# Two post norms of a transformer kernel: the residual turned ahead and the normed addend brought in by a product with a diagonal

## What is computed

```python
for layer in range(DEPTH_2):                 # 2
    h = rms_norm(x, mix_pre_g[layer])
    if layer < N_A:
        m = pool_mixer(h, pool_w[layer], pool_scale[layer])
    else:
        ...
        m = swa_sink_attention(q, kk, vv, sinks[j]) @ w_o[j]
    x = x + rms_norm(m, mix_post_g[layer])
    f = conv_glu_ffn(rms_norm(x, ffn_pre_g[layer]), ffn_w_in[layer], ffn_conv_w[layer],
                     ffn_conv_b[layer], ffn_w_out[layer])
    x = x + rms_norm(f, ffn_post_g[layer])
```

## Time and profile before

| | us |
|---|---|
| median of 3 runs | 882.49 |
| lowest, highest | 881.57, 883.0 |
| the profiled execution, device time | 882.28 |
| its span, first to last instruction | 880.4 |
| TensorE busy in the span | 854.7 (97%) |
| VectorE busy | 622.0 (71%) |
| ScalarE busy | 467.8 (53%) |
| GpSimd busy | 145.2 (16%) |
| mean granted clock of TensorE | 0.999 of full speed |

### The profile page before, as it was taken

How to read it: one execution, slowest core, us unless ns; L and a number is a source line. 1 busy time by engine, 2 the same in 40 slices (tenths; PEclk the granted TensorE clock), 3 DMA queues, 4 the chain that set the end, 5 groups by cost and what they waited for, 6 DMA issues and landing times.

```text
span 880.4 us, 15326 instructions
## 1 busy us (share of the span) xinstructions
PE 854.7 (97%) x5989; PEld 777.7 (88%) x5989; DVE 622.0 (71%) x816; ACT 467.8 (53%) x679; POOL 145.2 (16%) x132
## 2 busy tenths in 40 slices
PE   8999999998999999989999999999999999999997
PEld 8998888988999999869899999979766989999996
DVE  7887556779555555886876776877756677767776
ACT  5536765444444444465555554674656565455553
POOL 3282210017000000011122112000121121211200
PEclk9999999999999999999999999999999999999999
DMA  8953324634765555533555455435323235555541
GB/s 313 335 201 103 138 96 146 240 141 176 287 224 177 183 188 182 185 144 120 183 192 200 160 181 209 166 144 191 101 92 144 96 144 191 195 186 190 181 156 48
DMA packets 24088, 152.55 MB, mean 173 GB/s; under 512 B 2443, under 2 KB 3683, under 8 KB 7523
## 3 DMA queue, kind: packets, MB, share of 16 engines
q1 hardware_dynamic: 22672, 145.44, 47.1%
q10 hardware_dynamic: 1363, 6.37, 1.9%
HBM read 150.71 MB, written 1.09 MB: 172 GB/s over the span
## 4 chain that ended last, share of the span: by engine, by line
PE 64%; DVE 9%; ACT 3%; issue 2%; POOL 0%; DVEq 0%; POOLq 0%; ACTq 0%
PE up L990 12%; PE up L992 12%; PE up L991 12%; PE down L996 6%; PE down L997 6%; PE down L998 6%; DVE w_lo L1533 3%; PE up L1031 2%; PE down L1068 1%; PE down L1070 1%; DVE region L1949 1%; PE down L1458 1%; PE down L1216 1%; PE down L1074 1%; DVE mid L1808 1%
## 5 line engine op out<-in xcount | busy, mean ns | idle before, releaser
L1533 DVE TENSOR_TENSOR w_lo<-w,w_hi 128x2048 fp32r<-128x2048 f32 x133 | 316.8, 2387 | 63.6 <-ACT w_hi L641 63.5
L990 PE MATMUL up<-x_lo,w_hi 128*128 128x256 f32 x1240 | 354.1, 286 | 1.2 <-DVE w_lo L1533 1.2
L991 PE MATMUL up<-x_hi,w_hi 128*128 128x256 f32 x1240 | 350.8, 283 | 0.0
L992 PE MATMUL up<-x_hi,w_lo 128*128 128x256 f32 x1240 | 350.7, 283 | 0.0
L641 ACT ACTIVATE w_hi<-w 128x2048 fp32r<-128x2048 f32 x133 | 253.4, 1907 | 65.2 <-PE down L998 27.9
L990 PEld LDWEIGHTS up<-x_lo,w_hi 128*128 128x128 f32 x1240 | 237.7, 192 | 4.1 <-DVE w_lo L1533 2.1
L991 PEld LDWEIGHTS up<-x_hi,w_hi 128*128 128x128 f32 x1240 | 237.8, 192 | 1.2
L992 PEld LDWEIGHTS up<-x_hi,w_lo 128*128 128x128 f32 x1240 | 237.7, 192 | 0.0
L996 PE MATMUL down<-w_hi,mid 128*128 128x512 f32 x256 | 100.4, 392 | 3.2 <-DVE mid L1808 1.5
L997 PE MATMUL down<-w_hi,mid 128*128 128x512 f32 x256 | 100.0, 391 | 0.0
L998 PE MATMUL down<-w_lo,mid 128*128 128x512 f32 x256 | 99.6, 389 | 0.0
(11 more groups left out here) (246 smaller groups left out, 980.8 us busy)
## 6 DMA issues: line engine op xcount, KB each, us to landing
w<-w_stream SPq DMA_DIRECT2D x134, 1024.0 KB, 4.8
gates<-vec_store ACTq DMA_DIRECT2D x5, 1024.0 KB, 4.8
region<-rpb SPq DMA_DIRECT2D x2, 768.0 KB, 12.4
gates<-x_in SPq DMA_DIRECT2D x2, 512.0 KB, 3.8
result<-res SPq DMA_DIRECT2D x4, 256.0 KB, 2.0
con<-consts SPq DMA_DIRECT2D x1, 801.0 KB, 8.3
proj<-bands ACTq DMA_DIRECT2D x1, 544.0 KB, 3.7
gates<-vec_store ACTq DMA_DIRECT2D x1, 512.0 KB, 3.6
```

The costliest lines, as they stand in the source:

```text
L990: m(out_ap, w_hi[slot][:, w_cols:w_cols + P], xl, start=first, stop=False, skip_group_check=True)
L991: m(out_ap, w_hi[slot][:, w_cols:w_cols + P], xh, start=False, stop=False, skip_group_check=True)
L992: return m(out_ap, w_lo[slot][:, w_cols:w_cols + P], xh, start=False, stop=last, skip_group_check=True)
L1533: v.tensor_tensor(lo_of(n), w32[s][:, :], hi_of(n).bitcast(F32), ALU.subtract).then_inc(w_lo_ready, 1)
```

## The change

For the two post norms in `BY_DIAGONAL` the turned new residual is no longer the transpose of a sum that VectorE has made. TensorE makes the sum itself, in PSUM:
- `turn_old`: the old residual is turned by ordinary f32 products with the identity (residual chunk as the stationary operand), 16 of them. In `MIXPOST1` all 16 stand directly behind the last output product, in `MIXPOST0` between the others, since their banks are still being read.
- `diagonal(t)`: VectorE multiplies the identity by the roots of token half t, which gives `diag`, 128x128.
- `add_scaled`: the gained addend `s_tok` as stationary operand times `diag`, 16 products, accumulated onto the turned residual. `x_turned` is counted there.
- The dummy products of both places go.
- VectorE's additions into `res` (`added`) stand later in its queue: in `MIXPOST0` all four pieces behind `lower`; in `MIXPOST1` two ahead of it and two behind. They wait for `res_read`, after which TensorE no longer reads the old residual.
- ScalarE's squares of the new residual for the pre norm all stand behind the `x_hi` chunks for these two.
- In both gated layers: VectorE waits for the pre norm's root before the split of unit base + 2; the split of unit base + 3 moves from ahead of the first multiply to behind it; ScalarE's gelu of pair 0 moves ahead of the value half's product, and its split of unit base + 4 stands right behind that.

```diff
+        diag = sb("diag", [P, TT, P])
+        BY_DIAGONAL = (MIXPOST0, MIXPOST1)
...
+                if k_post not in BY_DIAGONAL:
+                    squares(0)
                 name, which = fills[0]
                 for c in range(DC):
...
-                for q in range(2):
-                    act.wait_ge(x_new, 4 * b + 2 + q + 1)
-                    mean_square(k_pre, 1, q, tok(res, 1, q), pre_squared)
+                if k_post in BY_DIAGONAL:
+                    squares(0)
+                squares(1)
...
-                    if kind == 0 and ends:
+                    if kind == 0 and (ends or j == 0):
                         gelu()
-                if not ends:
+                if j and not ends:
                     gelu()
...
+            def turned(c, t):
+
+                return turned_chunk(c)[:, t * P:(t + 1) * P]
+
+            def turn_old(c, last):
+
+                for t in range(TT):
+                    for k in (c, c + 1):
+                        ins = m(turned(k, t), res[:, t, k * P:(k + 1) * P], ident[:, :], start=(k == c and t == 0), stop=False,
+                                skip_group_check=True)
+                if last:
+                    ins.then_inc(res_read, 1)
+
+            def add_scaled(t, c):
+
+                for k in (c, c + 1):
+                    ins = m(turned(k, t), s_tok[:, t, k * P:(k + 1) * P], diag[:, t, :], start=False, stop=True,
+                            skip_group_check=True)
+                if t == 1:
+                    ins.then_inc(x_turned, 1)
+
+            def turn_scaled(k_post):
+
+                b, d = POST.index(k_post), TT * BY_DIAGONAL.index(k_post)
+                pe.wait_ge(post_gained, 4 * b + 2)
+                if k_post == MIXPOST0:
+                    turn_old(0, False)
+                    turn_old(2, False)
+                pe.wait_ge(diag_ready, d + 1)
+                add_scaled(0, 0)
+                add_scaled(0, 2)
+                pe.wait_ge(post_gained, 4 * b + 3)
+                if k_post == MIXPOST0:
+                    turn_old(4, False)
+                add_scaled(0, 4)
+                if k_post == MIXPOST1:
+                    add_scaled(0, 6)
+                pe.wait_ge(diag_ready, d + 2)
+                add_scaled(1, 0)
+                add_scaled(1, 2)
+                if k_post == MIXPOST1:
+                    pe.wait_ge(post_gained, 4 * b + 4)
+                add_scaled(1, 4)
+                pe.wait_ge(post_gained, 4 * b + 4)
+                if k_post == MIXPOST0:
+                    turn_old(6, True)
+                    add_scaled(0, 6)
+                add_scaled(1, 6)
...
-            keep_busy(aux, 13)
-            turn_new(MIXPOST0)
+            turn_scaled(MIXPOST0)
...
-            keep_busy(down[2], 6)
-            turn_new(MIXPOST1)
+            pe.wait_ge(p_ready, 32)
+            pe.wait_ge(pt_ready, 32)
+            for c in (0, 2, 4, 6):
+                turn_old(c, c == 6)
+            turn_scaled(MIXPOST1)
...
+                def diagonal(t):
+                    dve.wait_ge(rstd_ready, ROOT[k, t] + 1)
+                    v.tensor_scalar(diag[:, t, :], ident[:, :], stat[:, k, 2 + t:3 + t], None, ALU.mult)\
+                        .then_inc(diag_ready, 1)
...
+                gained(0, 0)
+                gained(0, 1)
                 if k == MIXPOST0:
-                    gained(1)
-                    added(0)
+                    gained(1, 0)
+                    diagonal(0)
+                    gained(1, 1)
+                    diagonal(1)
+                elif k == MIXPOST1:
+                    diagonal(0)
+                    variance(k, 1, (sq_ready, 4 * b + 4))
+                    gained(1, 0)
+                    diagonal(1)
+                    gained(1, 1, False)
...
             lower([("ffn_pre0", X_FFN0)])
+            added(MIXPOST0, 0)
+            added(MIXPOST0, 1)
...
+                    if kind == 0 and j == 0:
+                        next_split(at, base)
...
                 variance(k_pre, BOTH, (pre_squared, 4 * PRE.index(k_pre) + 8))
+                dve.wait_ge(rstd_ready, ROOT[k_pre, BOTH] + 1)
                 next_split(STRAIGHT, base - 1)
                 rows_out(k_pre)
-                next_split(STRAIGHT, base)
...
             post_sums(MIXPOST1, wo_bank, row_b, 1, (row_b_landed, 32))
+            added(MIXPOST1, 0)
             lower([("ffn_pre1", X_FFN1)])
+            added(MIXPOST1, 1)
```

More of the change, by code:

```diff
@@ L379, in build @@
         x_new = sem("x_new")
+        diag_ready = sem("diag_ready")
+        res_read = sem("res_read")
         pre_squared = sem("pre_squared")
@@ L839, in fill, with squares @@
                 b = POST.index(k_post)
-                for q in range(2):
-                    act.wait_ge(x_new, 4 * b + q + 1)
-                    mean_square(k_pre, 0, q, tok(res, 0, q), pre_squared)
+                def squares(t):
+                    for q in range(2):
+                        act.wait_ge(x_new, 4 * b + 2 * t + q + 1)
+                        mean_square(k_pre, t, q, tok(res, t, q), pre_squared)
+                if k_post not in BY_DIAGONAL:
+                    squares(0)
                 name, which = fills[0]
@@ L1126, in turn_new @@
                 turn_half(res, 0, 0, False)
-                if k_post != MIXPOST1:
-                    pe.wait_ge(post_gained, {MIXPOST0: 4, FFNPOST0: 8}[k_post])
+                pe.wait_ge(post_gained, 4 * b + 4)
                 pe.wait_ge(x_new, 4 * b + 2)
                 turn_half(res, 0, 1, False)
-                if k_post == MIXPOST1:
-                    keep_busy(wo_bank[0][0], 8)
                 pe.wait_ge(x_new, 4 * b + 3)
@@ L1901, in post_sums, with gained, added @@
                     dve.wait_ge(x_new, 4 * b)
[L1902 to L1914, removed]
-                if k == MIXPOST0:
-                    gained(1)
-                    added(0)
-                else:
-                    added(0)
-                    gained(1)
-                added(1)
+                def gained(t, q, root=True):
+                    dve.wait_ge(sq_ready, 4 * b + 2 * t + q + 1)
+                    if q == 1 and root:
+                        variance(k, t, (sq_ready, 4 * b + 2 * t + 2))
+                    v.tensor_tensor(tok(s_tok, t, q), banks[t][q][:, :], row_half(buf, which, q), ALU.mult)\
+                        .then_inc(post_gained, 1)
+                def diagonal(t):
[4 more added lines that the diff above has]
+                gained(0, 1)
+                if k == MIXPOST0:
+                    gained(1, 0)
[8 more added lines that the diff above has]
+                    gained(1, 1, False)
+                else:
+                    added(k, 0)
+                    gained(1, 0)
+                    gained(1, 1)
+                    added(k, 1)
+            def added(k, t):
+                if k in BY_DIAGONAL and t == 0:
+                    dve.wait_ge(res_read, BY_DIAGONAL.index(k) + 1)
+                dve.wait_ge(post_gained, 4 * POST.index(k) + 2 * t + 2)
+                add_normed(k, t)
             dve.wait_ge(h2_ready, 4)
```

## The result

| | before | after |
|---|---|---|
| median of 20 runs each | 882.63 | 884.01 |
| lowest, highest | 881.57, 885.23 | 883.50, 885.50 |
| profiled execution, device time | 882.28 | 883.50 |
| its span | 880.4 | 881.7 |
| TensorE busy in the span | 854.7 | 858.8 |

The ratio is 1.0017, with a 95% interval of 1.0011 to 1.0024: the changed kernel is slower by about 1.5 us. The forecast was 884.1. Every time used here is of an execution at a granted clock of 0.996 or more, where the clock is listed; two of the third experiment's ten ran at 0.66 and 0.56, took 1190 and 1395 us, and are left out.

The account below looks back on a forecast made before the run. TensorE, with slack in both post-norm windows before, becomes what ends them: +4.07 - 2.40 = +1.67 us on the profiled 882.28 is 883.95, with the runs' median 0.21 higher 884.1; range 882.2 to 886.7.

Parts of the forecast that it names:

- Both terms of the sum: TensorE's products in the two post norms cost +4.07 us; shorter VectorE chains in the gated layers give back 2.40.
- TensorE's products: Two post norms: 32 products at 0.222 us take 7.1 in each window, delaying `first_unit` by 2.20 and 1.87, together +4.07.
- No wait in the windows: Between the preceding products' end and `first_unit` in both norms, TensorE's new waits for gained pieces and diagonals cost 0.
- The second diagonal: First norm: its root ends at 393.11, the diagonal takes 0.3 us; TensorE asks at 395.3, so 2 us of cover.
- The chain after the row: Gated layers, from the row's copy to the first lower half's end: 14.72 us becomes 13.51, 1.2 shorter.
- The give-back: TensorE's stalls behind the windows, 1.27 us in one layer and 1.31 in the other: 2.40 of 2.58 comes back.
- the second stall: First gated layer: TensorE's next product could start at 425.96 but starts at 426.70, 0.74 us lost; second layer 0.78.
- the stalls: Sign of being right: TensorE's stalls before the first two sums of the gated layers would be under 0.1 us.
- The root: Pre norm's root takes 0.55 us, ends at 404.7; the split waiting for it leaves 0.8 and 1.1 us of cover.
- nothing is given back: Rival, chance 0.17: ScalarE's table load waits with the gelu for the first taps, 1.28 us eating the 1.20; 886.5.
- The transpose price for a product: Rival, chance 0.07: the post norms' products cost 0.105 us each, 3.4 for 32, so the kernel is faster, 876.5.
- The partial rival: Rival, chance 0.14: TensorE pays more, the root misses its 0.8 us cover, or a product costs 0.237; 885.3.

Follow-up runs that it names:

- the third experiment: Changed kernel with its 32 turns of the old residual as transposes instead of products with the identity (output wrong, run for time alone): 880.02, ratio 0.9975.
- The first experiment: Kernel before with only the new order at the start of the two gated layers; residual, transposes and dummy products as before: 880.04, ratio 0.9977.

## Why the prediction was right

The change measured is +1.4 us by the medians and +1.5 by the ratio, against +1.67 forecast. That 884.1 and 884.01 agree to 0.1 us is in part luck: the kernel before has 882.63 as the median of 20 runs, 0.14 more than the three runs that the forecast stood on. The ratio lies just inside the 0.2% that the prediction took as the least that can be told, as the likeliest time did, though the prediction gave "slower" a little more chance than "same". The interval, 1.0011 to 1.0024, does not reach 1: small as it is, the loss is real. Both terms of the sum were right in mechanism and size.

**TensorE's products (+4.07 forecast, +4.02 measured).** The price was taken as 0.222 and is 0.221 (7.06 us for 32). No wait in the windows was late. The second diagonal was ready at 393.4 against 395.3 needed, as worked out; it took 0.29 against my 0.3. Three runs bear on this term: more products cost their full price, transposes in their place give the difference back, and the products without the order cost what the two windows grew by (4.02 us, against 3.7 by the medians and 4.1 by the ratio).

**The chain after the row (1.2 shorter forecast, 1.27 measured).** The chain is 13.51 forecast and 13.45 measured. The step that holds the gain is the one named, the split that covers ScalarE's product (the split put back gives 14.63). The gelu's move I had taken as harmless and not as a gain, and so it is. GpSimd's product went from 1.30 to 3.3 beside the split, as forecast, and VectorE's split was first by 0.14 us. VectorE's row, then GpSimd's:

```profile
416.31 2.29 DVE L1590 TENSOR_TENSOR w_lo<-w,w_hi 128x2048 fp32r<-128x2048 f32 x1
```

```profile
416.45 3.30 POOL L611 TENSOR_TENSOR region<-region 128x512 f32<-128x512 f32 x1 [11.71 <-DVE region L2027]
```

The Trainium skill's page "SBUF — State Buffer", section "SBUF: two separate sides", says that of these two engines the one that starts first keeps the shared port pair for its whole instruction and the other is blocked. The trace agrees: VectorE's split ends at 416.31 + 2.29 = 418.60, and GpSimd's product, which started second, ends 1.15 us after that, about the 1.30 that it takes when VectorE is idle. In the run without the wait for the root, the root (404.33, 2.68 us) likewise ends 0.55 after the split beside it (404.17 + 2.29).

**The give-back (2.40 forecast, 2.51 measured).** VectorE's chain, and not TensorE, still sets the end of the second stall: from the copy of the row to the next tile's first product are 19.87 us (407.69 to 427.56) against 21.13 (405.57 to 426.70), 1.26 shorter, and the second layer has the same two lengths. Twice 1.26 is what came back. One sign that I had named did not come: the stalls were to be under 0.1, and the second keeps 0.21 and 0.20, where the forecast left 0.07 and 0.11. I had kept the sum's own length, 420.34 to 425.96, but 5.62 us of it held the slow start of a product after an idle time (its successor started 0.35 later, the others 0.23); without the stall the sum takes 421.88 to 427.35, 5.47. So TensorE asks for the next split 0.15 sooner than I had it and waits that much longer for it, which changes the stall that is left and not the time.

**The root.** It ended at 404.74 (404.7 forecast), but took 0.70 and not 0.55 us. The split that waits for it left 0.63 us of cover ahead of the row and 0.94 in the second layer (0.8 and 1.1 forecast), so the wait cost nothing, as said.

**The rivals.** That nothing is given back needed the table load behind the wait. In the changed kernel it starts at once behind ScalarE's product, and the gelu waits for the taps without it:

```profile
409.99 1.28 ACT L888 ACT_TABLE_LOAD   x1
412.78 0.63 ACT L888 ACTIVATE region<-region 128x512 f32<-128x512 f32 x1 [1.51 <-DVE region L2027]
```

With the gelu put back, load (415.13) and ACTIVATE (416.43) follow each other within 0.02 us; the load costs its 1.28 us and nothing more. The Trainium skill's page "ScalarE: Activation LUTs", section "What ACT_TABLE_LOAD costs", adds a drain of about 1.38 us for every switch; no run here shows one, and the measurement decides. The transpose price for a product falls by the third experiment, which shows both prices side by side. The partial rival named a product at 0.237 and a root past its cover; neither came.

**What I had not seen.** The prediction treated the change as one thing. It is two that work each without the other, one that costs 3.7 to 4.1 us and one that gives 2.0 to 2.5, and the question whether the second works without the first wasn't put. The first experiment was the most useful for that reason.

**Open.** Why a sum begun by transposes and continued by products comes out wrong in the third experiment was not looked into; nor was whether the transposes could be added onto the products. The order alone gives 2.5 us by the starts in its trace and 2.2 by the medians; the difference is within the spread of the runs and was not followed up.

## What to carry to other kernels

Moving work to an engine that stands idle at a wait is free only up to the length of that wait: count its instructions at their price (here 32 x 0.221 against 4.9 and 5.2 us) before taking work off another engine's path, and move only as much as fits. Where an engine waits for a neighbour's short instruction, look in its own queue for something long that stands just ahead of the instruction that feeds the neighbour; put behind it, it fills the wait (here a split of 2.28 us over a wait of 1.17). And when a change bundles two ideas, run each alone: here the one that paid was a reordering of a few lines.

## What the runs showed of the hardware

- An ordinary f32 product of 128x128 takes TensorE 0.219 to 0.223 us back to back (two loads, two passes), with the residual or the addend as the stationary operand; a transpose of the same block takes 0.109.
- An f32 product of 128x512 on GpSimd with both inputs in SBUF takes 1.30 us alone and 3.1 to 3.3 when it starts just after a VectorE subtraction with two SBUF inputs. Delaying it until VectorE was idle cost nothing in the end (884.27 against 884.01).
- The reciprocal root of 128x2 numbers on GpSimd took 0.70 us undisturbed and 2.68 beside a VectorE split; one of 128x1 took 0.55.
- A table load on ScalarE takes 1.28 us. It starts while the operand of the activation behind it is still to come (409.99, for a gelu that starts at 412.78), so it can lie in a wait.
- After an idle time of 0.4 us TensorE's next product starts its successor 0.35 us later instead of 0.23 (products of 128x512).
